# The entry of the first layer: constants cut up, x's norm from a token-major copy, products of ones during the load

## The chip, the cores and the metric

The kernel runs on one core of a Trainium2 chip. The metric is the device time of one execution in microseconds, lower is better. TensorE multiplies, VectorE (DVE), ScalarE (ACT) and GpSimd (POOL) work on vectors, SyncE (SP) issues the DMAs that move data between HBM and the on-chip memory.

## What is computed

Two blocks of a network over 256 tokens of width 2048, in f32. The entry, which the change touches, is the first block's norm and input product (`a_w_in`), a causal convolution of width 4, and the gated recurrence's decay, whose constants come from `a_lam`. The second block uses softmaxed bounds from `hgrn_lb_logits`, and conditions `silu(c)`, `silu(c_ctx)`.

```python
u = x * lax.rsqrt(mean(x * x, -1) + 1e-6) * norm_pre     # first block's norm
xb, gate = split(u @ a_w_in)                             # 2048 -> 2 x 2048
xc = causal_conv(xb, conv_w) + conv_b                    # width 4
r, i = sigmoid(block_matmul(xc, w_r) + b_r), sigmoid(block_matmul(xc, w_i) + b_i)
log_a = -8 * softplus(-lam) * r                          # decay of the recurrence
...                                                      # scan, gate, output, second block
mod = silu(c) @ w_mod + b_mod;  lb = softmax(hgrn_lb_logits)
```

## The kernel before

Activations lie feature-major: 128 features on the partitions, 256 tokens along, 16 such tiles for x (`XT`). A weight comes in blocks of 128 x 1024 (512 KB) into a ring of seven (`WF`), loaded by SP in the order of use. Each block is split in two: ScalarE rounds it to the high part (`WH`, function `high`), VectorE subtracts for the low part (`WL`, `low_part`); four buffers each. The moving operand is split the same way (`UX`, by `make`). TensorE does three products for each tile of 128 x 128: high x high, high x low, low x high. A WF buffer is free for its next load when VectorE has made the low part (`w_lo`); WH and WL are free when TensorE has finished the block (`prod`). Below, a block's number counts from 0 in the order of use: WL 4 is the low part of block 4.

One list of steps, made by `timetable()`, is walked by each engine's program; an engine takes from it what is its own, in order, and semaphores hold it where another's result is needed. Between two engines nothing else sets the order. The list begins with the loads of x in five pieces between weights, then the parameters and constants (`load_params`).

The first product is a quad: the first four output tiles of `xb` together, over blocks 0 to 7, two tiles of x for each block (`linear_quad`). x is multiplied by the gain `norm_pre` alone; the norm's factor 1/rms of each token, `RX` (the same on all partitions), is applied when an output tile is evacuated: `tt(XB, ps, RX, mult)` by VectorE. So no evacuation can be done before RX, and tile xb 4 needs the bank of the quad's first tile. Then follow xb 4 and xb 5 (blocks 8 to 11), the gates' products (blocks 12, 13), xb 6 (blocks 14, 15), with four products of a modulation block (`in_mod`, operand `SM`) ahead of it. Each xb tile has, after its evacuation, an activation on ScalarE (the fourth convolution tap and bias), three taps on VectorE, and a split for the gates (`XCs`).

RX before: in the quad's steps `x_square`, ScalarE squares four tiles of x at a time (128 x 1024), GpSimd adds the four to one (`XPARTS`), and in the step `("recip", "x")` TensorE multiplies ones with the four sums, which adds over features and spreads the sum to all partitions; ScalarE takes the root, VectorE the reciprocal of 128 x 256.

Small constants before: `small_params`, a background task of VectorE and ScalarE, in steps after the quad. It makes the softplus of -lam with a series (`nsp`, `psp`) and the softmaxed bounds (`lb`, `oml`), all on 128 x 16. In the step `conditions` ScalarE takes the sigmoid of `c` and VectorE multiplies (`cf`). ScalarE loads a table of functions when the function asked for is not in the present one.

Of the kernel before, what the change touches and what calls it, by code (L numbers as in the profile page):

```python
# [25 lines left out]
    ("norm_pre", 16), ("norm_post", 16), ("conv_w", 64), ("conv_b", 16), ("b_r", 16), ("b_i", 16),  # L26
    ("lam", 16), ("c", 16), ("cc", 16), ("b_mod", 96), ("npm", 16), ("nqm", 16), ("npl", 16),
    ("nql", 16), ("dw_w", 31 * 8), ("dw_b", 8), ("ln_g", 8), ("ln_b", 8), ("lb", 32), ("hng", 8),
]
PCOL = {}  # L30
_at = 0
for _n, _w in PARAMS:
# [8 lines left out]
    ["x", "y1", "x2", "ctx", "cmean", "cvar", "ro0", "ro1", "ro2", "ro3", "y2", "x3", "out"])}  # L41
# [5 lines left out]
PARTS_OF = {"small_params": 6, "recurrence": 16, "prepare_ctx": 26, "conv_branch": 46, "conv_split": 8,  # L47
# [17 lines left out]


# [3 lines left out]
def timetable():  # L70
# [287 lines left out]
    def linear_quad(kind, js):  # L358
# [14 lines left out]
        for b in range(8):  # L373
# [35 lines left out]
    for kind, j in order:  # L409
# [151 lines left out]
def build(nc, ctx, ins, out):  # L561
# [7 lines left out]
    def sem(name):  # L569
# [31 lines left out]
    ones_ok, c_sig, cf_ok, x_sq, x_part, mk_ok = (  # L601
        sem(n) for n in ("ones_ok", "c_sig", "cf_ok", "x_sq", "x_part", "mk_ok"))
# [69 lines left out]
    XT, CT, PT, BIG = area(0, 16), area(24, 16), area(56, 2), area(64, 16)  # L672
# [8 lines left out]
    XPARTS = area(82, 4)  # L681
# [32 lines left out]
    warm = small(4)  # L714
# [50 lines left out]
    ST = {"x": (RX, T, D), "y1": (RSTD[0], T, D), "x2": (RSTD[0], T, D), "ctx": (RC, T, D), "cvar": (SQ[1], T, 1024),  # L765
# [11 lines left out]
    def sync_program(sync):  # L777
# [3 lines left out]
        for what, *a in steps:  # L781
            if what == "start":
                n = PCOL["norm_pre"] + 16
                sync.dma_start(PR[:, 0:n], ins["params"][:, 0:n]).then_inc(s_gain, 16)
# [3 lines left out]
            elif what == "load_params":  # L788
                n = PCOL["norm_pre"] + 16
                sync.dma_start(PR[:, n:], ins["params"][:, n:]).then_inc(s_par, 16)  # L790
                sync.dma_start(CN[:, :], ins["consts"]).then_inc(s_par, 16)
            elif what == "load":
                i = a[0]
                b = blocks[i]
                if i >= NF:
                    w.wait_ge(*freed(i - NF))
                sync.dma_start(WF[:, i % NF, :], ins[b["name"]][b["index"]][:, b["lo"]:b["lo"] + BLK]).then_inc(
                    landed[i % NF], 16)
            elif what == "load_late":
                w.wait_ge(st_rs, RECIP["x"])  # L800
# [21 lines left out]
    def tensor_program(tensor):  # L822
# [70 lines left out]
        def stat(name):  # L893
            n = STAT[name]
            w.wait_ge(st_sq, n - 1)
            if name == "x":
                w.wait_ge(ones_ok, 1)
                for q in range(4):
                    w.wait_ge(x_part, q + 1)
                    i = mm(bank[7][:, 0:T], ONES[:, :], XPARTS[:, q, :], q == 0, q == 3)  # L900
            elif name == "ctx":
# [15 lines left out]
            i.then_inc(st_mm, 1)  # L917

# [148 lines left out]
        for what, *a in steps:  # L1067
# [8 lines left out]
            elif what == "stat" or (what == "recip" and a[0] == "x"):  # L1076
# [10 lines left out]
    def scalar_program(scalar):  # L1087
# [50 lines left out]
        def square(group, ft, src):  # L1138

            if ft == 0:  # L1140
                w.wait_ge(st_sq, {0: STAT["x"], 1: STAT["y1"], 2: STAT["ro3"], 3: STAT["y2"]}[group])
# [161 lines left out]
        def small_params(_):  # L1303
            w.wait_ge(sp_v, 1)
            act(el, al, ACT.Exp, scale=-1.0).then_inc(sp_a, 1)
            for _ in range(4):
                yield
            w.wait_ge(sp_v, 2)
            act(le, le, ACT.Exp).then_inc(sp_a, 1)
            yield  # L1310
            yield

# [128 lines left out]
        for what, *a in steps:  # L1441
# [8 lines left out]
            elif what == "bg":  # L1450
                name = a[0]
                if a[1] == 1:
                    running[name] = {
                        "small_params": small_params, "recurrence": recurrence, "prepare_ctx": prepare_ctx,
# [26 lines left out]
            elif what == "start":  # L1481
                w.wait_ge(ones_ok, 1)
                act(warm[:, 0:1], ONES[:, 0:1], ACT.Sqrt)
            elif what == "x_square":
                q = a[0]
                for k in range(4 * q, 4 * q + 4):
                    w.wait_ge(s_x[piece_of(k)], 16)
                act(BIG[:, 4 * q:4 * q + 4, :], XT[:, 4 * q:4 * q + 4, :], ACT.Square).then_inc(x_sq, 1)
            elif what == "conditions":
                w.wait_ge(s_par, 32)  # L1490
                act(cs, PR[:, PCOL["c"]:PCOL["c"] + 32], ACT.Sigmoid).then_inc(c_sig, 1)

    def vector_program(vector):
# [150 lines left out]
        def evac(what):  # L1644
            kind, j = what
            ps, leave = psum(what), left(what)[0]
            if kind == "xb":
                w.wait_ge(*full(what))
                w.wait_ge(st_rs, RECIP["x"])
# [109 lines left out]
        def small_params(_):  # L1759
            w.wait_ge(s_par, 32)  # L1760
            mark(ts(nl, lam, -1.0, None, ALU.mult))
            marked()
            tt(al, nl, lam, ALU.max).then_inc(sp_v, 1)
            w.wait_ge(sp_a, 1)
            mark(ts(sl, el, 2.0, None, ALU.add))
            marked()
            mark(vector.reciprocal(sl, sl))
            yield
            marked()
            mark(tt(sl, sl, el, ALU.mult))  # L1770
# [416 lines left out]
```

## Time and profile before

| | us |
|---|---|
| median of 3 runs | 2148.67 |
| lowest, highest | 2148.39, 2149.68 |
| span of the profiled execution | 2146.7 |
| TensorE busy in it | 2101.1 (98%) |
| VectorE, ScalarE, GpSimd busy | 1592.8, 1026.9, 99.5 |

The profiled execution is one of its own; its time is given as the span from its first instruction to its last. A line of a timeline gives the start, the time from there to the end of the group, engine and source line, the operation with output <- inputs, the number of instructions merged, and in brackets how long the engine stood idle before and what ended that. A window's last three numbers are the granted TensorE clock as a share of 2.4 GHz, DMA's busy share, and GB/s.

### The profile page before, as it was taken

How to read it: one execution, taken by the hardware profiler on the slowest of the kernel's cores; microseconds unless marked ns; L12 is line 12 of the kernel's file. 1: busy time of each engine (PE TensorE's matmuls, PEld its weight loads, DVE VectorE, ACT ScalarE, POOL GpSimd, SP SyncE). 2: the span in 40 equal slices, each digit the busy share in tenths (PEclk: the TensorE clock that was granted, in tenths of full speed). 3: DMA queues.
4: the chain of work that ended last, by engine and by line, in shares of the span. 5: the costliest groups of instructions: out<-in, count | busy, mean ns of one | idle time of the engine just before them, and what ended most of it. 6: DMA issues, size and time to landing. Idle time of an engine off the chain costs nothing.

```text
span 2146.7 us, 31802 instructions
## 1 busy us (share of the span) xinstructions
PE 2101.1 (98%) x12800; PEld 1830.9 (85%) x12800; DVE 1592.8 (74%) x2357; ACT 1026.9 (48%) x1560; POOL 99.5 (5%) x81
## 2 busy tenths in 40 slices
PE   7999999999999999999999999999999999999997
PEld 7787799787888888899999888878888888888886
DVE  7778699698889777667877898576766766656655
ACT  5766344556532322555554455554444434434443
POOL 1000002020000000000000001210000000000012
PEclk9999999999999999999999999999999999999998
DMA  6556778676733567444346988645775765555552
GB/s 232 197 200 224 249 253 274 223 273 230 247 111 130 172 234 267 149 132 141 132 135 207 367 300 300 228 146 195 258 254 187 240 230 196 181 192 196 187 178 97
DMA packets 122402, 447.80 MB, mean 209 GB/s; under 512 B 13712, under 2 KB 13840, under 8 KB 121872
## 3 DMA queue, kind: packets, MB, share of 16 engines
q1 hardware_dynamic: 122256, 445.78, 61.1%
q8 instruction: 101, 1.65, 0.3%
q14 instruction: 45, 0.37, 0.1%
HBM read 441.53 MB, written 4.19 MB: 208 GB/s over the span
## 4 chain that ended last, share of the span: by engine, by line
PE 71%; DVE 2%; ACT 1%; issue 1%; POOL 0%; POOLq 0%; DVEq 0%; ACTq 0%
PE bank L826 70%; DVE WL L1499 0%; DVE AR L1506 0%; PE bank L955 0%; DVE SR L1506 0%; PE bank L986 0%; ACT WH L1093 0%; DVE AR L1499 0%; POOL AR L2102 0%; ACT AR L1094 0%; ACT AR L1093 0%; DVE AR L1599 0%; ACT SR L1094 0%; POOL AR L2104 0%; ACT L1094 0%
## 5 line engine op out<-in xcount | busy, mean ns | idle before, releaser
L826 PE MATMUL bank<-SR,WH 128*128 128x512 f32 (+1 forms) x6880 | 1811.5, 352 | 28.6 <-DVE WL L1499 10.7
L826 PE MATMUL bank<-SR,WL 128*128 128x256 f32 (+1 forms) x5088 | 1208.7, 288 | 0.5 <-DVE SR L1506 0.4
L826 PEld LDWEIGHTS bank<-SR,WH 128*128 128x128 f32 x6880 | 1096.0, 190 | 94.0 <-issue 30.6
L826 PEld LDWEIGHTS bank<-SR,WL 128*128 128x128 f32 x5088 | 963.7, 190 | 156.1 <-DVE SR L1506 1.9
L1499 DVE TENSOR_TENSOR WL<-WF,WH 128x1024 fp32r<-128x1024 f32 x636 | 774.6, 1229 | 221.2 <-ACT WH L1093 221.0
L1093 ACT ACTIVATE WH<-WF 128x1024 fp32r<-128x1024 f32 x636 | 671.6, 1057 | 463.4 <-PE bank L826 428.0
L1093 ACT ACTIVATE AR<-bank 128x256 f32<-128x256 f32 (+2 forms) x261 | 103.6, 407 | 277.8 <-PE bank L826 263.4
L1506 DVE SCALAR_TENSOR_TENSOR AR<-WF,SM,AR 128x512 f32<-128x512 f32 (+1 forms) x240 | 232.8, 1000 | 4.5
L1499 DVE TENSOR_TENSOR AR<-AR 128x256 f32<-128x256 f32 (+9 forms) x374 | 154.8, 445 | 58.4 <-ACT AR L1094 35.4
L2097 POOL TENSOR_TENSOR AR<-AR 128x256 f32<-128x256 f32 x56 | 74.2, 1325 | 2013.1 <-ACT AR L1094 2012.8
L1499 DVE TENSOR_TENSOR AR<-AR,bank 128x256 f32<-128x256 f32 x112 | 47.2, 421 | 119.2 <-PE bank L826 91.2
L1094 ACT ACTIVATE AR<-AR 128x256 f32<-128x256 f32 (+3 forms) x152 | 75.1, 499 | 96.3 <-DVE AR L1499 81.3
L1499 DVE TENSOR_TENSOR AR<-bank,AR 128x256 f32<-128x256 f32 (+1 forms) x200 | 86.0, 432 | 39.9 <-PE bank L826 18.0
L1506 DVE SCALAR_TENSOR_TENSOR AR<-AR,PR 128x255 f32<-128x255 f32 (+21 forms) x200 | 89.1, 448 | 6.0
L1093 ACT ACTIVATE SR<-AR 128x256 fp32r<-128x256 f32 (+1 forms) x138 | 56.5, 419 | 71.5 <-DVE AR L1499 64.6
L1094 ACT ACTIVATE AR<-bank 128x256 f32<-128x256 f32 x74 | 26.6, 382 | 118.8 <-PE bank L826 118.7
L826 PE MATMUL bank<-WF,SM 128*2 128x512 f32 x160 | 73.4, 592 | 0.0
L1499 DVE TENSOR_TENSOR SR<-AR,SR 128x256 fp32r<-128x256 f32 (+1 forms) x138 | 58.9, 435 | 16.4 <-ACT SR L1093 15.7
L826 PE MATMUL bank<-AR 128*128 128x128 f32 (+1 forms) x416 | 64.0, 297 | 2.8 <-issue 2.3
L826 PEld LDWEIGHTS bank<-AR 128*128 128x128 f32 x416 | 56.7, 191 | 5.0 <-issue 2.7
L826 PEld LDWEIGHTS bank<-WF,SM 128*2 128x2 f32 x160 | 11.2, 84 | 39.6 <-issue 36.3
L1506 DVE SCALAR_TENSOR_TENSOR AR<-AR 128x256 f32<-128x256 f32 x88 | 37.3, 423 | 8.8 <-ACT AR L1094 6.6
(75 smaller groups left out, 464.0 us busy)
## 6 DMA issues: line engine op xcount, KB each, us to landing
WF<-in_mlp SPq DMA_DIRECT2D x256, 512.0 KB, 4.2
WF<-in_mod SPq DMA_DIRECT2D x192, 512.0 KB, 4.9
WF<-in_w_in SPq DMA_DIRECT2D x176, 512.0 KB, 4.3
WF<-in_a_in SPq DMA_DIRECT2D x64, 512.0 KB, 4.7
WF<-in_a_out SPq DMA_DIRECT2D x32, 512.0 KB, 5.1
WF<-in_ple_g SPq DMA_DIRECT2D x32, 512.0 KB, 4.5
WF<-in_w_out SPq DMA_DIRECT2D x32, 512.0 KB, 5.6
WF<-in_pw SPq DMA_DIRECT2D x16, 512.0 KB, 3.2
```

The lines of the kernel that those rows point to most:

```text
L826: return tensor.matmul(o, l, r, start=start, stop=stop, skip_group_check=True)
L1093: return scalar.activation(o, x, f, scale=scale)
L1094: return scalar.activation(o, x, f, scale=scale, bias=bias)
L1499: return vector.tensor_tensor(o, a, b, op)
L1506: return vector.scalar_tensor_tensor(o, a, s, b, op1, op2)
L2097: pool.tensor_tensor(ACC, ACC, SQ[ft % 2], ALU.add).then_inc(acc, 1)
```

## The change

- `PARAMS` is reordered: gain, `c`, `cc`, `lam` and `lb` come first, and the first parameter load brings 96 columns (48 KB) instead of 16 (8 KB).
- `small_params` is gone as a task. `small(0)` stands at the start, ahead of the first split, with both exponentials on ScalarE there; `small(1)` to `small(6)` stand between the quad's blocks 0 to 5.
- x comes a second time, token-major (`xR`, 128 x 4096, 2 MB), loaded in the quad's first block step. ScalarE squares each half with a sum along the row (`accum_out`, 128 x 2048) in the steps of blocks 5 and 6. A new step `x_scale` behind the quad: root of 128 x 2 on ScalarE, reciprocal of 128 x 2 on VectorE, two products on TensorE of the factor, repeated, with the identity, which spread it to all partitions, and a copy to RX on ScalarE.
- GpSimd's eight additions, the four products with ones, the root and the reciprocal of 128 x 256 are gone.
- At the start TensorE multiplies ones by ones 14 times (128 x 128, f32, `WARM`).
- The table of the exponential is loaded first, the root's ahead of the first square, the sigmoid's at `conditions`, and it stays for the gates. The product `cf` moves behind xb 4 (`conditioned`).

```diff
-            background.append(("small_params", 0))
...
+                if b == 0:
+                    steps.append(("load_xr",))
+                if b < 6:
+                    steps.append(("small", b + 1))
+                if b in (5, 6):
+                    steps.append(("x_square", b - 5))
-                if b < 4:
-                    steps.append(("x_square", b))
-                if b == 6:
-                    steps.append(("recip", "x"))
...
+        if kind == "xb":
+            steps.append(("x_scale",))
...
+            if j == 4:
+                steps.append(("conditioned",))
...
+        def x_wider():                                   # TensorE
+            w.wait_ge(x_inv, 1)
+            w.wait_ge(s_par, 32)
+            for h in range(2):
+                r = xinv[:, h:h + 1]
+                r = bass.AP(tensor=r.tensor, offset=r.offset, ap=[r.ap[0], [0, P]])
+                i = mm(bank[7][:, h * P:h * P + P], r, ident, True, True)
+            i.then_inc(x_wide, 1)
...
+            elif what == "start":                        # TensorE
+                w.wait_ge(ones_ok, 1)
+                for _ in range(WARM):
+                    mm(bank[7][:, 0:P], ONES[:, :], ONES[:, :], True, True)
...
-                act(warm[:, 0:1], ONES[:, 0:1], ACT.Sqrt)
+                act(warm[:, 0:1], ONES[:, 0:1], ACT.Exp)
+                w.wait_ge(sp_v, 1)
+                act(el, al, ACT.Exp, scale=-1.0)
+                act(le, le, ACT.Exp).then_inc(sp_a, 1)
...
+                h = a[0]                                 # x_square, ScalarE
+                if h == 0:
+                    act(warm[:, 4:5], ONES[:, 0:1], ACT.Sqrt)
+                w.wait_ge(s_xr, 16)
+                scalar.activation(XR[:, h, :], XR[:, h, :], ACT.Square, scale=1.0, bias=0.0,
+                                  accum_out=xsum[:, h:h + 1]).then_inc(x_sq, 1)
+            elif what == "x_scale":
+                w.wait_ge(s_par, 32)
+                w.wait_ge(x_sq, 2)
+                act(xsum, xsum, ACT.Sqrt, scale=1.0 / D, bias=eps).then_inc(x_root, 1)
+                w.wait_ge(x_wide, 1)
+                act(RX, bank[7][:, 0:T], ACT.Copy).then_inc(x_rs, 1)
...
-                w.wait_ge(st_rs, RECIP["x"])             # VectorE, evacuation of xb
+                w.wait_ge(x_rs, 1)
...
+            elif what == "x_scale":                      # VectorE
+                w.wait_ge(x_root, 1)
+                vector.reciprocal(xinv, xsum).then_inc(x_inv, 1)
```

VectorE behind the quad. `SM` are the small constants, `AR` with `PR` a convolution tap (its width 255, 254 or 253), `WL` a low part, `AR<-bank,AR` an evacuation. Before:

```order
L1502 TENSOR_SCALAR SM<-SM 128x16
L1506 SCALAR_TENSOR_TENSOR SM<-SM 128x16 x8
L1502 TENSOR_SCALAR SM<-SM 128x16
L1506 SCALAR_TENSOR_TENSOR SM<-SM 128x16
L1502 TENSOR_SCALAR SM<-SM 128x16 x2
L1499 TENSOR_TENSOR SM<-PR 128x16
L1499 TENSOR_TENSOR SM<-PR,SM 128x2x8
L1499 TENSOR_TENSOR WL<-WF,WH 128x1024
L1506 SCALAR_TENSOR_TENSOR AR<-AR,PR 128x255
```

Now, at the same low part and on:

```order
L1526 SCALAR_TENSOR_TENSOR AR<-AR,PR 128x253
L1519 TENSOR_TENSOR WL<-WF,WH 128x1024
L1526 SCALAR_TENSOR_TENSOR AR<-AR,PR 128x255
L1526 SCALAR_TENSOR_TENSOR AR<-AR,PR 128x254
L1526 SCALAR_TENSOR_TENSOR AR<-AR,PR 128x253
L1526 SCALAR_TENSOR_TENSOR AR<-AR,PR 128x255
L1526 SCALAR_TENSOR_TENSOR AR<-AR,PR 128x254
L1526 SCALAR_TENSOR_TENSOR AR<-AR,PR 128x253
L1519 TENSOR_TENSOR AR<-bank,AR 128x256
L1519 TENSOR_TENSOR SM<-SM,PR 128x32
L1519 TENSOR_TENSOR WL<-WF,WH 128x1024
```

The constants are gone from between the taps and WL 11, and `cf` (`SM<-SM,PR 128x32`) now stands behind the evacuation of xb 4.

ScalarE from the end of the quad. `SR<-AR,PR` casts a tile of x, `WH` is a high part, `AR<-bank,CN` the root of the sum, `AR<-AR,PR ... x4` the four convolution activations. Before:

```order
L1093 ACTIVATE SR<-AR,PR 128x256 x2
L1093 ACTIVATE WH<-WF 128x1024
L1094 ACTIVATE AR<-bank,CN 128x256
L1093 ACTIVATE WH<-WF 128x1024
L1094 ACTIVATE AR<-AR,PR 128x256 x4
L1094 ACT_TABLE_LOAD
L1094 ACTIVATE SM<-PR 128x32
L1093 ACTIVATE WH<-WF 128x1024
L1094 ACT_TABLE_LOAD
L1094 ACTIVATE SM<-SM 128x16
```

Now:

```order
L1113 ACT_TABLE_LOAD
L1113 ACTIVATE SM<-ONES 128x1
L1504 ACTIVATE AR,SM<-AR 128x2048
L1112 ACTIVATE SR<-AR,PR 128x256 x2
L1112 ACTIVATE WH<-WF 128x1024
L1504 ACTIVATE AR,SM<-AR 128x2048
L1112 ACTIVATE WH<-WF 128x1024
L1113 ACTIVATE SM<-SM,CN 128x2
L1112 ACTIVATE AR<-bank 128x256
L1113 ACTIVATE AR<-AR,PR 128x256 x4
L1113 ACT_TABLE_LOAD
L1113 ACTIVATE SM<-PR 128x32
```

A table load and two squares of 128 x 2048 now stand in this stretch, and the table load behind `SM<-PR 128x32` is gone.

SP, from the last piece of x. Before:

```order
L787 DMA AR<-in_xT 128x1024
L790 DMA PR<-in_params 128x648
L791 DMA CN<-in_consts 128x132
L797 DMA WF<-in_a_in 128x1024 x7
L797 DMA WF<-in_a_gates 128x1024 x2
```

Now:

```order
L795 DMA AR<-in_xT 128x1024
L797 DMA PR<-in_params 128x568
L798 DMA CN<-in_consts 128x132
L804 DMA WF<-in_a_in 128x1024 x4
L807 DMA AR<-in_xR 128x4096
L804 DMA WF<-in_a_in 128x1024 x3
```

The 2 MB of xR stand between blocks 8 and 9 on the same queue.

## Rows read from the trace of the kernel before

**Rows 1.** Windows: length, busy us (instructions) of each engine, clock, DMA.
```profile
0.00:75.00 75.00, 57.86 (x398) 52.79 (x399) 52.83 (x96) 48.99 (x78) 10.23 (x13) 0.95 0.60 209
75.00:2147.00 2072.00, 2043.27 (x12405) 1778.13 (x12403) 1540.00 (x2261) 977.94 (x1483) 89.24 (x68) 1.00 0.61 209
```

**Rows 2.** Waits of TensorE, 0 to 75: us in total, times, longest.
```profile
PE bank L826 <- DVE WL L1499: 7.5, 5, 3.6
```

**Rows 3.** Timeline, TensorE, 50 to 72: start, us, work, count, idle before.
```profile
50.98 0.80 PE L826 MATMUL bank<-SR,WH 128*128 128x256 f32 x2 [3.63 <-DVE WL L1499]
...
57.12 0.48 PE L826 MATMUL bank<-SR,WH 128*128 128x256 f32 x2 [0.65 <-DVE SR L1499]
...
60.94 0.50 PE L826 MATMUL bank<-SR,WH 128*128 128x256 f32 x2 [1.43 <-DVE AR L1499]
...
64.66 0.47 PE L826 MATMUL bank<-SR,WH 128*128 128x256 f32 x2 [0.94 <-DVE WL L1499]
...
70.57 1.88 PE L826 MATMUL bank<-WF,SM 128*2 128x512 f32 x4
```

**Rows 4.** Windows, 52 to 54, all engines.
```profile
52.00:54.00 2.00, 2.00 (x11) 2.00 (x11) 1.80 (x5) 0.09 (x1) 0.00 (x0) 0.50 0.77 242
```

**Rows 5.** Timeline, VectorE, 38 to 61.
```profile
38.75 0.42 DVE L1499 TENSOR_TENSOR AR<-bank,AR 128x256 f32<-128x256 f32 x1 [0.29 <-PE bank L826]
41.38 0.19 DVE L1499 TENSOR_TENSOR SM<-SM,PR 128x32 f32<-128x32 f32 x1 [2.21 <-ACT SM L1094]
...
42.63 2.95 DVE L1506 SCALAR_TENSOR_TENSOR AR<-AR,PR 128x255 f32<-128x255 f32 x6
45.49 0.17 DVE L1502 TENSOR_SCALAR SM<-PR 128x16 f32<-128x16 f32 x1
...
49.71 1.22 DVE L1499 TENSOR_TENSOR WL<-WF,WH 128x1024 fp32r<-128x1024 f32 x1
...
53.70 0.17 DVE L1499 TENSOR_TENSOR SM<-PR,SM 128x16 f32<-128x16 f32 x1
...
55.42 1.22 DVE L1499 TENSOR_TENSOR WL<-WF,WH 128x1024 fp32r<-128x1024 f32 x1
...
60.47 0.42 DVE L1499 TENSOR_TENSOR AR<-bank,AR 128x256 f32<-128x256 f32 x1
```

**Rows 6.** Timeline, ScalarE, 37 to 66.
```profile
37.05 2.76 ACT L1094 ACTIVATE AR<-AR,PR 128x256 f32<-128x256 f32 x4
...
62.79 1.28 ACT L1094 ACT_TABLE_LOAD   x1
64.09 1.57 ACT L1094 ACTIVATE AR<-bank,PR 128x256 f32<-128x256 f32 x4
```

**Rows 7.** Timeline, VectorE, 8 to 14.
```profile
8.66 0.88 DVE L1506 SCALAR_TENSOR_TENSOR SR<-AR,PR,SR 128x256 fp32r<-128x256 f32 x2
11.23 2.08 DVE L1506 SCALAR_TENSOR_TENSOR SR<-AR,PR,SR 128x256 fp32r<-128x256 f32 x2 [1.70 <-ACT SR L1093]
13.23 1.21 DVE L1499 TENSOR_TENSOR WL<-WF,WH 128x1024 fp32r<-128x1024 f32 x1
```

**Rows 8.** DMA issues at 3.06 and 14.47 (KB, us to landing); window 15 to 20.
```profile
AR<-in_xT SPq DMA_DIRECT2D x1, 512.0 KB, 7.0
...
WF<-in_a_in SPq DMA_DIRECT2D x1, 512.0 KB, 8.5
...
15.00:20.00 5.00, 3.87 (x32) 3.67 (x32) 4.38 (x4) 2.58 (x5) 2.11 (x2) 1.00 1.04 408
```

**Rows 9.** Groups by form, ScalarE: busy us, mean ns, idle before.
```profile
L1093 ACT ACTIVATE WH<-WF 128x1024 fp32r<-128x1024 f32 x636 | 671.6, 1057 | 463.4 <-PE bank L826 428.0 <-DMA WF<-in_w_out 14.5 <-DMA WF<-in_ple_g 8.9
...
L1093 ACT ACTIVATE SR<-AR,PR 128x256 fp32r<-128x256 f32 x16 | 7.2, 494 | 3.0 <-DMA AR<-in_xT 3.0
...
L1094 ACT ACTIVATE AR<-AR 128x2048 f32<-128x2048 f32 x2 | 3.8, 1917 | 6.7 <-DVE AR L1502 5.9 <-DVE AR L1499 0.9
```

**Rows 10.** Timeline, TensorE, 31 to 33: the products with ones.
```profile
31.07 1.89 PE L826 MATMUL bank<-AR,ONES 128*128 128x256 f32 x8
```

More of the change, by code:

```diff
@@ L40 @@
 STAT = {n: i + 1 for i, n in enumerate(
-    ["x", "y1", "x2", "ctx", "cmean", "cvar", "ro0", "ro1", "ro2", "ro3", "y2", "x3", "out"])}
+    ["y1", "x2", "ctx", "cmean", "cvar", "ro0", "ro1", "ro2", "ro3", "y2", "x3", "out"])}
 RECIP = {n: i + 1 for i, n in enumerate(n for n in STAT if n != "cmean")}
@@ L712, in build @@
     gsc, gscc, gga, gsf, ggf = (small(16) for _ in range(5))
-    warm = small(4)
+    warm = small(5)
+    xsum, xinv = small(2), small(2)
     def bank_of(what):
@@ L895, in stat @@
             w.wait_ge(st_sq, n - 1)
[L896 to L901, printed above, removed]
+            if name == "ctx":
                 w.wait_ge(cx_v, 1)
@@ L1075, in tensor_program @@
                 next(running[name], None)
-            elif what == "stat" or (what == "recip" and a[0] == "x"):
+            elif what == "start":
[3 more added lines that the diff above has]
+            elif what == "x_scale":
+                x_wider()
+            elif what == "stat":
                 stat(a[0])
@@ new lines, in small @@
+            if n == 0:
+                w.wait_ge(s_gain, 16)
+                mark(ts(nl, lam, -1.0, None, ALU.mult))
+                mark(tt(lm3, l4[:, :, 0, :], l4[:, :, 1, :], ALU.max))
+                marked()
+                tt(al, nl, lam, ALU.max)
+                tt(le4[:, :, 0, :], l4[:, :, 0, :], lm3, ALU.subtract)
+                tt(le4[:, :, 1, :], l4[:, :, 1, :], lm3, ALU.subtract).then_inc(sp_v, 1)
+            elif n == 1:
+                w.wait_ge(sp_a, 1)
+                mark(ts(sl, el, 2.0, None, ALU.add))
+                mark(tt(lb3, le4[:, :, 0, :], le4[:, :, 1, :], ALU.add))
+                marked()
+                vector.reciprocal(sl, sl)
+                mark(vector.reciprocal(lb, lb))
+            elif n == 2:
+                tt(sl, sl, el, ALU.mult)
+                mark(tt(lb3, lb3, le4[:, :, 0, :], ALU.mult))
+                marked()
+                tt(s2, sl, sl, ALU.mult)
+                mark(ts(oml, lb, -1.0, 1.0, ALU.mult, ALU.add))
+            elif n == 3:
+                mark(ts(ql, s2, 1.0 / 17, None, ALU.mult))
+                marked()
+                mark(stt(ql, ql, 1.0 / 15, s2, ALU.add, ALU.mult))
+                marked()
+                mark(stt(ql, ql, 1.0 / 13, s2, ALU.add, ALU.mult))
+            elif n == 4:
+                for k in (5, 4, 3):
+                    mark(stt(ql, ql, 1.0 / (2 * k + 1), s2, ALU.add, ALU.mult))
+                    marked()
+            elif n == 5:
+                for k in (2, 1):
+                    mark(stt(ql, ql, 1.0 / (2 * k + 1), s2, ALU.add, ALU.mult))
+                    marked()
+                ts(nl, nl, 0.0, None, ALU.max)
+                mark(stt(ql, ql, 1.0, sl, ALU.add, ALU.mult))
+            else:
+                mark(stt(ql, ql, 2.0, nl, ALU.mult, ALU.add))
+                marked()
+                ts(nsp, ql, -8.0, None, ALU.mult)
+                ts(psp, ql, 8.0, None, ALU.mult).then_inc(sp_ok, 1)
@@ L2058, in vector_program @@
                 vector.tensor_copy(MK[:, :, :], MF).then_inc(mk_ok, 1)
-            elif what == "conditions":
+            elif what == "conditioned":
                 w.wait_ge(c_sig, 1)
                 tt(cf, cs, PR[:, PCOL["c"]:PCOL["c"] + 32], ALU.mult).then_inc(cf_ok, 1)
+            elif what == "start":
+                small(0)
+            elif what == "small":
+                small(a[0])
+            elif what == "x_scale":
+                w.wait_ge(x_root, 1)
+                vector.reciprocal(xinv, xsum).then_inc(x_inv, 1)
             elif what == "finish":
```

111 lines of the change are left out of this document (27 added, 84 removed).

## The prediction

> **What bounds the kernel now.** First the windows [rows 1]: after 75 us TensorE is busy 2043.27 of 2072 us, 98.6%, so what is off TensorE there costs little. Before 75 us it is busy 57.86 of 75, and all of the change lies there. Then the waits of TensorE in that stretch [rows 2]: the split of the weights' low parts (WL, VectorE) holds it five times for 7.5 us, the longest 3.6. In order of time [rows 3], with a weight's block at 2.9 us (48 matmuls of xb 6 from 64.66 to 70.57, so 24 in 2.95, nearer 2.88 without the ends): 3.63 us of idleness before 50.98, 0.65 before 57.12, 1.43 before 60.94, 0.94 before 64.66. Behind the longest of them the granted clock is 0.50 [rows 4], the 1.2 GHz level: the block that starts at 50.98 takes until about 56.5, 2.6 us more than at 2.4 GHz.
>
> Why WL is late is read from VectorE's queue [rows 5]. It has evacuated the quad's last tile at 39.2 and then stands 2.21 us until 41.38, behind the product cf, which waits for ScalarE's sigmoid, itself behind four activations (2.76 us, until 39.8) and the load of a table, 1.28 us [rows 6]. Then come a WL and six convolution taps, and from 45.49 to 49.71, 4.22 us, nothing but 16-column operations on constants: a chain of about twenty instructions, each waiting for the one before. Only then WL for the block that TensorE wants, which begins at 49.71. From 53.70 to 55.08 (it ends with the evacuation ahead of 55.42, 0.34 us) another 1.38 us of constants. TensorE at 60.94 follows the evacuation that VectorE began at 60.47, to 0.05 us: here VectorE's queue is the path, and TensorE follows it.
>
> **The constants.** They are cut into seven pieces that stand between the splits of the quad. Out of the stretch from 39.2 to 55.42 (16.2 us) go 2.21 + 4.22 + 1.38 = 7.8 us; cf moves behind the evacuation of xb 4, its sigmoid then long done, and costs 0.1 there. In their new places six pieces of two to four operations cost VectorE 0.6 to 0.9 us each (4.22 us for 19 operations is 0.2 each). Below I count them where they stand. ScalarE's two exponentials move ahead of the first x piece, for which it waits until about 5.2 now, and the constants' first piece needs about 1 us after a load of 48 instead of 8 KB, so I take 0 and at most 0.5.
>
> **The entry to the quad.** GpSimd's eight sums go. While one ran, two of VectorE's 256-column operations took 2.08 us instead of 0.88 [rows 7], and the second WL began at 13.23. Without the sums and without ScalarE's four squares of 1.04 us, those two operations follow x's third piece (landed at 3.06 + 7.0 = 10.1 [rows 8]), so WL 1 ends near 12.7 (before: 14.4). Next in turn: WL 2 at 16.7, WL 4 at 22.7, WL 5 at 23.8. Blocks on TensorE then end at 15.6, 19.6, 22.5, 25.6 (block 4), 28.5, 31.4 and 34.3 (block 7). The four f32 products with ones, 1.89 us on TensorE [rows 10], are no longer there; with them and the later waits block 7 ended at about 38.4. The fourteen products of ones at the start last 14 x 0.43 = 6.0 us at 1.2 GHz (0.43 is a quarter of 1.89 us doubled for the clock and halved for 128 columns), from 0.95 to 7.0, before TensorE's first weight at 7.53. They let block 0 end at 10.5 instead of 12.9; block 1 starts at 12.7 either way, so I give them 0.2 us. If the clock falls again in the new pause, block 1 takes 2.9 us more, ends at 18.5 and moves block 2 by 1.8 us; the next waits swallow most of that.
>
> **x's scale, the new path.** xR is 2 MB on the queue that weights use. It is issued behind the ninth weight block, which landed at 14.47 + 8.5 = 23.0 in a stretch at 408 GB/s [rows 8]; the same bytes stand ahead of it, so xR lands at 23.0 + 2.10 MB / 408 = 28.1. The weights behind it land 5.1 us later, the tenth at 28.1 + 1.3 = 29.4, wanted at 30.8: covered. ScalarE's queue, with WH at 0.95 from start to start and two x casts 0.8 [rows 9]: WH 8 waits for block 4 and starts at 25.65; table load 1.28 [rows 6] and a one-column root to 28.0; square with sum over 2048 columns 28.15 to 30.0 (a plain square of 2048 takes 1.92 [rows 9], the sum itself I price at 0, upper bound 0.3 each); casts of x 14 and 15 to 30.8, in time for block 7 at 31.4; WH 9 to 31.75; second square to 33.6; WH 10 to 34.55; root 34.75. VectorE's reciprocal to 35.05, two products with the identity 0.6, a copy 0.4: RX is ready at 36.15. TensorE stands from 34.3 to 35.1 for the reciprocal and from 35.7 to 36.65 for the first evacuation. The first evacuation thus starts at 36.2; before it was four evacuations back from 39.2, at 36.6. All that the quad gained on TensorE, 4 us, shrinks to 0.4 here.
>
> The Trainium skill speaks against the table load in that chain: *ScalarE: Activation LUTs*, section "What ACT_TABLE_LOAD costs", gives 1.28 us and a drain of 1.38 us on top. The trace has no such drain: the load of 1.28 us at 62.79 is followed by an activation that starts at 64.09 [rows 6]. By the page the chain would end 1.4 us later; I keep the row.
>
> **The sum.** From 36.2 VectorE does four evacuations back to back (0.34 each, 1.35; before they were paced by TensorE, 2.6), a WL 1.15, six taps 2.9, and meets WH 11: ScalarE needs 2.76 + 1.29 + 0.1 + 1.05 for four activations, the sigmoid's table, the sigmoid and WH, from 36.65 to 41.85; VectorE is there at 41.6 and waits 0.25. WL, six taps, one evacuation and cf: WL 12 starts at 46.25, before at 55.42 [rows 5]. That is 9.2 us. From there to 60.94 both kernels have the same queue, so TensorE resumes at 51.75. TensorE's own work allows it: from 36.65 four blocks end at 48.2, and it wants VectorE's next cast at 48.1. Last, the 0.94 us before 64.66. The row names a WL [rows 3], but that one ended at 63.7; the product also needs a bank that ScalarE frees, whose first sigmoid starts at 64.09 and ends at 64.5, behind a table load at 62.79 [rows 6]. I read it as that. The sigmoid's table is now in place, the load goes, and TensorE resumes as soon as its four products of 1.88 us end at 63.72: 0.94 us more. Together 10.1 us; the 3.63 and the 0.50 clock are part of it, not to be added. What is late next: evacuations again, then ScalarE's recurrence around 70 to 85, which moves by 10.5 us along with TensorE, and where TensorE is fully busy. Span 2146.7 - 10.1 = 2136.6. The median of the runs is 2148.67, 2.0 above the span: 2138.6.
>
> **Rivals.**
> (a) *xR comes late.* Each microsecond by which it lands after 28 passes to the end whole, since the sum hangs on RX from there. For it: it shares the queue; against it: the stretch ran at 408 GB/s. At 200 GB/s it lands at 33.5 and the gain is 4.7: 2144. The sums and the drain of the page, if they exist, are of this kind, 0.3 to 2 us: 2139 to 2141.
> (b) *The gain is given back.* TensorE, 10 us ahead, would meet a wait it did not have: weights behind xR (needs landing over 1.4 us later than I have for the tenth block), or ScalarE at 70 to 85, where it is busy all the time. A gain under 4.3 us: 2145 to 2149.
> (c) *Slower.* One mechanism: RX is so late that ScalarE, which waits in order for xR, holds up the casts and WH 9 behind it; TensorE starves at block 7, falls to 1.2 GHz for some 5.5 us as after 50.98 and loses 2.7 us more. Loss begins when xR lands later than 28 + 10.1 - 2.7 = 35.5, a transfer below 170 GB/s. At 40: 2153. Nothing in the rows points there.
> (d) *More.* If WL 1 and WL 2 come earlier than I have them, ScalarE's chain starts earlier, but xR bounds it at 28.1: at most 0.5. If TensorE's later idleness (29 us after 75) also shrinks, up to 3: 2135.5.
> (e) *The warm-up does nothing.* As worked out, 0.2 us at most; no case of its own.
>
> **How the numbers follow.** Forecast (gain 8.5 to 11.5) 0.66; (d) 0.07; (a) with a gain of 4.3 to 8.5: 0.18; (b) 0.06; (c) 0.03. A measurement of this kernel can tell about 0.2%, 4.3 us, from no change. Faster by that: 0.66 + 0.07 + 0.18 = 0.91; within: 0.06; slower: 0.03. Range: 2135.5, the end of (d), to 2143.0, xR at 32.5; that leaves out (b), (c) and the tail of (a).
>
> **What would show it.** In the profile after: no idle stretch of TensorE over 2 us after 20 us and granted clock 1.00 from 45 to 60; xR landing near 28; RX's copy near 36; WL 12 on VectorE at 46.2; TensorE's first evacuation wait in the gates ending at 51.75 and the mod products of xb 6 directly followed by its weights near 54.5. Wrong would be: the copy of RX after 38, a wait of TensorE for WH or WL between 20 and 34, or a new wait at 60 to 75.

## The result

The changed kernel takes 2139.28 us (median of 4 runs, 2139.09 to 2139.71) where the one before, beside it, takes 2149.18 (4 runs, 2148.39 to 2150.12). The ratio is 0.9953, 95% interval 0.9939 to 0.9967. The profiled execution's span fell from 2146.7 to 2137.2 us, 9.5 us; 10.1 were forecast, and the time of 2138.6 was missed by 0.7. Nearly everything was at its place. The experiments show how the gain divides: the constants and the sigmoid's table bring most of it, as the forecast had it (8.7 of 10.1 us), and the new norm by itself brings nothing that the medians show, which the forecast did not say.

The same two windows as in [rows 1], of the changed kernel:

```profile
0.00:75.00 75.00, 67.86 (x488) 61.70 (x489) 51.56 (x109) 53.82 (x87) 0.41 (x5) 0.98 0.72 261
75.00:2147.00 2072.00, 2033.74 (x12339) 1770.15 (x12337) 1532.72 (x2248) 971.61 (x1474) 88.78 (x68) 0.99 0.61 208
```

TensorE is busy 10.0 us more of the first 75, 5.7 of which are the products of ones (first row below), and 9.5 us less behind them, where the stretch simply ends earlier. Its longer idle stretches up to 60 us, as in [rows 3]:

```profile
0.99 5.69 PE L835 MATMUL bank<-ONES 128*128 128x128 f32 x28 [0.99 <-POOL ONES L2103]
...
13.22 0.80 PE L835 MATMUL bank<-SR,WH 128*128 128x256 f32 x2 [3.11 <-DVE WL L1519]
...
35.95 0.71 PE L835 MATMUL bank<-CN,SM 128*128 128x128 f32 x4 [0.87 <-DVE SM L2087]
37.75 0.48 PE L835 MATMUL bank<-SR,WH 128*128 128x256 f32 x2 [1.09 <-DVE AR L1519]
...
52.45 0.50 PE L835 MATMUL bank<-SR,WH 128*128 128x256 f32 x2 [0.79 <-DVE AR L1519]
...
53.36 1.88 PE L835 MATMUL bank<-WF,SM 128*2 128x512 f32 x4
55.17 0.50 PE L835 MATMUL bank<-SR,WH 128*128 128x256 f32 x2
```

The 3.63 us before 50.98 are gone; what is left of the gates' waits is 0.79 before 52.45, where before 60.94 it was 1.43. The product of xb 6 follows the modulation's products without a pause, at 55.17 instead of 64.66: 9.49 us, the whole difference of the spans. VectorE, whose queue is the path ([rows 5] of before):

```profile
35.73 0.17 DVE L2087 RECIPROCAL SM<-SM 128x2 f32<-128x2 f32 x1 [1.22 <-ACT SM L1113]
37.18 1.42 DVE L1519 TENSOR_TENSOR AR<-bank,AR 128x256 f32<-128x256 f32 x4 [1.29 <-ACT AR L1112]
38.52 1.21 DVE L1519 TENSOR_TENSOR WL<-WF,WH 128x1024 fp32r<-128x1024 f32 x1
39.65 2.94 DVE L1526 SCALAR_TENSOR_TENSOR AR<-AR,PR 128x255 f32<-128x255 f32 x6
...
46.84 0.18 DVE L1519 TENSOR_TENSOR SM<-SM,PR 128x32 f32<-128x32 f32 x1
46.94 1.22 DVE L1519 TENSOR_TENSOR WL<-WF,WH 128x1024 fp32r<-128x1024 f32 x1
```

WL 12 starts at 46.94 instead of 55.42. ScalarE, on the new path to RX:

```profile
26.35 1.06 ACT L1112 ACTIVATE WH<-WF 128x1024 fp32r<-128x1024 f32 x1 [1.02 <-PE bank L835]
27.43 1.28 ACT L1113 ACT_TABLE_LOAD   x1
28.72 0.20 ACT L1113 ACTIVATE SM<-ONES 128x1 f32<-128x1 f32 x1
28.91 1.91 ACT L1504 ACTIVATE AR<-AR 128x2048 f32<-128x2048 f32 x1
30.73 0.19 ACT L1504 ACTIVATION_READ_ACCUMULATOR AR<-AR 128x1 f32 x1
...
35.41 0.28 ACT L1113 ACTIVATE SM<-SM,CN 128x2 f32<-128x2 f32 x1
36.70 0.38 ACT L1112 ACTIVATE AR<-bank 128x256 f32<-128x256 f32 x1 [1.00 <-PE bank L835]
```

**A mark far behind the entry.** From 75 us on TensorE's waits are alike in both kernels. One of them, 1.78 us long, stands in every trace at about 1300 us, and the time at which TensorE resumes there tells what the entry has brought, without what comes later. Before and after:

```profile
1302.81 0.47 PE L826 MATMUL bank<-SR,WH 128*128 128x512 f32 x1 [1.79 <-issue]
```

```profile
1293.30 0.47 PE L835 MATMUL bank<-SR,WH 128*128 128x512 f32 x1 [1.78 <-issue]
```

That is 9.51 us. Below this is called the mark. In three executions of the changed kernel it stood at 1293.30, 1293.33 and 1293.73, with the first evacuation within 0.07 us (37.18, 37.13, 37.11): in the third the clock from 37 to 60 us was 0.93 instead of 1.00. So a difference of two marks under about 0.4 us says nothing by itself. Each mark below is that of one execution.

### The profile page after: what moved, and what is told of

It is laid out like the page before. It is cut to its first block, busy times and chain, and to the rows that moved or that the text cites. A ratio compares the mean times of both kernels' runs of the same rounds, so it can differ in the third digit from the quotient of the medians.

```text
span 2137.2 us, 31842 instructions
## 1 busy us (share of the span) xinstructions
PE 2101.6 (98%) x12824; PEld 1831.8 (86%) x12824; DVE 1584.3 (74%) x2357; ACT 1025.4 (48%) x1561; POOL 89.2 (4%) x73
## 4 chain that ended last, share of the span: by engine, by line
PE 71%; DVE 2%; ACT 1%; issue 1%; POOL 0%; POOLq 0%; ACTq 0%; DVEq 0%
PE bank L835 70%; DVE WL L1519 0%; DVE AR L1526 0%; DVE SR L1526 0%; PE bank L968 0%; ACT WH L1112 0%; PE bank L999 0%; DVE AR L1519 0%; POOL AR L2122 0%; ACT AR L1113 0%; ACT AR L1112 0%; DVE AR L1619 0%; ACT SR L1113 0%; POOL AR L2124 0%; ACT L1113 0%
## 5 line engine op out<-in xcount | busy, mean ns | idle before, releaser
L1113 ACT ACTIVATE AR<-AR 128x256 f32<-128x256 f32 (+2 forms) x148 | 70.9, 484 | 97.3 <-DVE AR L1519 82.5
L835 PEld LDWEIGHTS bank<-WF,SM 128*2 128x2 f32 x160 | 11.2, 84 | 39.6 <-issue 36.3
```

Source lines behind the costliest of these rows:

```text
L835: return tensor.matmul(o, l, r, start=start, stop=stop, skip_group_check=True)
L1113: return scalar.activation(o, x, f, scale=scale, bias=bias)
```

## The experiments

They were run in three groups, each on one chip, and each ratio is to the kernel before in the same group. The changed kernel itself was in two of the groups: 2138.93 us (4 runs, 2138.01 to 2141.37; before 2149.74) and 2139.55 (5 runs, 2139.07 to 2140.15; before 2148.30). Two variants, the table loaded once more and GpSimd's additions put back, have one execution each, so for them there is no median.

**The changed kernel again, in the first and in the last group:**

> The changed kernel again, beside the three that follow, so that they are compared on the same chip. 2139.3 within 0.4; ratio to before 0.9955.

> The changed kernel again, as the reference of this call: 2138.5 to 2139.7.

The ratios are 0.9951 (0.9937 to 0.9966) and 0.9958 (0.9944 to 0.9971), the marks 1293.73 and 1293.33. The profiled execution of the first has a span of 2139.2, 2 us more than the other's 2137.4; the last part of this section comes back to that. It is also the slowest run of its group, 2141.37 in time, and lies outside the 0.4 that was expected.

**The products of ones.**

```diff
-WARM = 14
+WARM = 0
```

> The changed kernel without the fourteen products of ones. Theory: they bring nothing, since block 1 waits for WL 1 (13.2 us) in either case and RX waits for xR. In the trace of the changed kernel the clock fell back to 1.2 GHz in the pause of 3.1 us before 13.22, so without them block 0 runs at 1.2 GHz (ends near 12.3) and block 1 at 2.4 GHz (ends near 16.1 instead of 17.4); both are absorbed by xR. Same time within 0.3 us as the changed kernel. Rival: the warm clock is worth the 3 us that block 0 is shorter: 2142.

Measured 2139.20 us (4 runs, 2138.57 to 2139.76) beside 2138.93, ratio 0.9951 (0.9936 to 0.9966), mark at 1293.52. Without the ones block 0 runs at half the clock, its first 16 products in 3.75 us instead of 2.18, and block 1 still starts at 13.12 instead of 13.22, as WL 1 sets it:

```profile
7.41 3.75 PE L835 MATMUL bank<-SR,WH 128*128 128x256 f32 x16 [7.41 <-ACT WH L1112]
...
13.12 0.64 PE L835 MATMUL bank<-SR,WH 128*128 128x256 f32 x2 [0.25 <-DVE WL L1519]
```

The ones bring nothing: what they save in block 0 becomes the 3.11 us of waiting. In the first execution of the changed kernel the products behind that pause run at the lower clock, until about 16 us, as these windows show; the last columns are the granted clock, DMA's share and GB/s:

```profile
10.00:15.00 5.00, 1.89 (x9) 1.78 (x9) 2.72 (x8) 4.17 (x7) 0.00 (x0) 0.77 1.01 406
15.00:20.00 5.00, 5.00 (x40) 5.00 (x40) 3.32 (x7) 1.91 (x3) 0.00 (x0) 0.89 1.04 412
```

That fall is not what makes the ones useless. In the execution with the mark at 1293.73 the clock stayed at 1.00 behind a pause of 3.00 us; TensorE then waited 0.42 us for the next WL, and the first evacuation came no earlier (37.11), since the squares waited for xR.

**The constants and the sigmoid's table alone.** Put on the kernel before: the reordered parameters, the seven pieces of `small`, the exponentials and their table at the start, `cf` behind xb 4. The norm stays with ScalarE's squares, GpSimd's sums, the products with ones and the root of 128 x 256.

```diff
+                if b < 6:
+                    steps.append(("small", b + 1))
                 if b < 4:
                     steps.append(("x_square", b))
+                if b == 4:
+                    steps.append(("root_table",))
...
-                background.append(("small_params", 0))
...
+            if j == 4:
+                steps.append(("conditioned",))
```

> The kernel before with the constants alone moved: seven pieces in the quad, exponentials first, the root's table loaded after block 4, the sigmoid's kept for the gates; norm by GpSimd and products with ones as before, no xR, no ones. Theory: the constants carry 7.8 us and the table 0.9, so 8.5 to 9.3 us under before, span near 2137.9, time near 2140; VectorE starts WL 12 near 47.6. Rival: the quad's entry needed the rebuilt norm to have room on VectorE for the pieces, and block 7 ends 2 us or more later than 38.5: gain of 6 to 7.

Measured 2139.56 us (4 runs, 2139.54 to 2140.39), ratio 0.9954 (0.9937 to 0.9970): in the median all but 0.6 us of the change's gain (2138.93 beside it), and within its spread. By the mark, 1294.63, it is 8.2 of 9.5 us: WL 12 starts at 48.21 instead of 55.42, 7.2 us earlier, and the 0.94 before xb 6 is gone. What 7.2 lacks to 7.8 is lost in the quad: three operations of the constants (27.01, 1.13 us) stand ahead of a split for which TensorE waits 0.77 us, its block starts at 28.81 instead of 28.12, and the last evacuation at 39.44 instead of 38.75 [rows 5].

```profile
37.66 0.77 DVE L1498 TENSOR_TENSOR AR<-bank,AR 128x256 f32<-128x256 f32 x2
...
39.44 0.42 DVE L1498 TENSOR_TENSOR AR<-bank,AR 128x256 f32<-128x256 f32 x1 [0.29 <-PE bank L830]
39.78 1.22 DVE L1498 TENSOR_TENSOR WL<-WF,WH 128x1024 fp32r<-128x1024 f32 x1
```

The first evacuation is 0.48 us later than in the changed kernel, and the four take 2.12 us to the next WL instead of 1.34, as TensorE is still finishing the quad's tiles. Together 1.26 us: that is what the new norm, with the ones and without GpSimd's additions, adds here (1.3 at the mark).

**The norm alone.** The reverse: the changed kernel with `small_params` as a background task, the tables and the exponentials as before. xR, the new scale and the ones stay.

```diff
-                if b < 6:
-                    steps.append(("small", b + 1))
...
+                background.append(("small_params", 0))
...
-            if j == 4:
-                steps.append(("conditioned",))
...
-                act(warm[:, 0:1], ONES[:, 0:1], ACT.Exp)
+                act(warm[:, 0:1], ONES[:, 0:1], ACT.Sqrt)
```

> The changed kernel with the constants made as before, as a task behind the quad, with their exponentials there; xR, the rebuilt norm and the ones stay. Theory: RX and the first evacuation stay near 37.2 (before 36.6), cf waits for the sigmoid until 41.3 as before, and 4.2 + 1.4 us of constants stand in VectorE's queue again, so TensorE waits before WL 11 until about 51 and the whole gain is gone: 2148.5 to 2150. Rival: the rebuilt norm is worth something of its own by TensorE's four microseconds in the quad: 2145 or less.

Measured 2148.38 us (10 runs) beside 2148.64 (19 runs), ratio 0.9999 (0.9990 to 1.0008). The mark is at 1302.22, 0.6 earlier than before. The expectation held, and its rival (2145 or less) did not. VectorE shows why so little is left:

```profile
36.76 1.42 DVE L1523 TENSOR_TENSOR AR<-bank,AR 128x256 f32<-128x256 f32 x4 [1.29 <-ACT AR L1109]
40.87 0.19 DVE L1523 TENSOR_TENSOR SM<-SM,PR 128x32 f32<-128x32 f32 x1 [2.69 <-ACT SM L1110]
```

The evacuations are done a microsecond earlier than before, and `cf`, behind them, waits for ScalarE's sigmoid 2.69 us instead of 2.21 [rows 5]. Half of the microsecond is left: WL 12 starts at 54.90 for 55.42. The old queue swallows the rest of what the new norm gives. Marks of the two halves add to 8.8 of 9.5 us.

**The table loaded once more.** The changed kernel, with an exponential that nobody needs behind xb 4, so that the sigmoid's table must be loaded again ahead of the gates' sigmoids.

```diff
+            elif what == "conditioned":
+                act(warm[:, 0:1], ONES[:, 0:1], ACT.Exp)
```

> The changed kernel with one activation of the exponential on ScalarE after xb 4 is evacuated, which costs a table load in ScalarE's idle time there and makes the sigmoid's table load return ahead of the gates' first sigmoid. Theory: TensorE resumes after the modulation products 0.7 to 0.95 us later than in the changed kernel, whose blocks follow them without a pause; span 0.7 to 0.95 longer, if the clock does the same elsewhere. Rival: the wait there was for WL 14, as the trace's releaser says: no change.

One execution: span 2139.3, mark 1295.55, 2.25 us later. Two waits of TensorE make it up:

```profile
53.74 0.51 PE L835 MATMUL bank<-SR,WH 128*128 128x256 f32 x2 [2.11 <-DVE AR L1521]
...
57.46 0.47 PE L835 MATMUL bank<-SR,WH 128*128 128x256 f32 x2 [0.93 <-DVE WL L1521]
```

The first is a side effect of the extra exponential (1.28 us of table load ahead of a WH, so 1.29 later than 52.45). The second is the pause of 0.94 us before 64.66 [rows 3] come back, 0.93 us. As in [rows 3] the row names a WL, yet that WL ended at 56.44, a microsecond before TensorE resumed. What ends just before 57.46 is the first sigmoid, behind its table:

```profile
55.59 1.28 ACT L1113 ACT_TABLE_LOAD   x1
56.89 1.57 ACT L1113 ACTIVATE AR<-bank,PR 128x256 f32<-128x256 f32 x4
```

**GpSimd's additions put back.** The changed kernel, with eight additions of GpSimd on an area that nobody uses (zeroed at the start), released by the same splits as before.

```diff
+        for q in range(4):
+            w.wait_ge(n_hi, (4, 6, 10, 12)[q])
+            pool.tensor_tensor(J[:, 0:2, :], J[:, 2:4, :], J[:, 4:6, :], ALU.add).then_inc(p_own, 1)
+            w.wait_ge(p_own, 2 * q + 2)
+            pool.tensor_tensor(J[:, 6, :], J[:, 0, :], J[:, 1, :], ALU.add).then_inc(p_own, 1)
```

> The changed kernel with eight additions on GpSimd of the sizes of before, on an area of zeros, released by the casts of x 3, 5, 9 and 11. Their sums go nowhere. Theory: VectorE's paired operations under them take about 2.1 us instead of 0.9 and a WL 2.3 instead of 1.2, TensorE's blocks 1 to 6 come up to 3 us later, and RX, bound by xR, stays within 1 us of 37.1: the end moves by under 1 us. Rival: the removed sums are a term of the gain: 2 us or more.

One execution: span 2138.1, mark 1295.15. VectorE's first evacuation is at 39.05, 1.87 us later than 37.18, and the mark 1.85 later: they are one and the same. The span is only 0.9 longer, since the stretch behind the mark was 1.0 shorter here. While GpSimd adds, VectorE's operations take longer (the last two rows are a GpSimd addition and ScalarE's first square):

```profile
12.01 2.29 DVE L1519 TENSOR_TENSOR WL<-WF,WH 128x1024 fp32r<-128x1024 f32 x1
...
21.98 4.01 DVE L1519 TENSOR_TENSOR WL<-WF,WH 128x1024 fp32r<-128x1024 f32 x2
25.91 2.12 DVE L1526 SCALAR_TENSOR_TENSOR SM<-SM 128x16 f32<-128x16 f32 x3
...
24.98 2.17 POOL L2110 TENSOR_TENSOR AR<-AR 128x512 f32<-128x512 f32 x1
...
30.80 1.90 ACT L1504 ACTIVATE AR<-AR 128x2048 f32<-128x2048 f32 x1
```

against 1.22, 2.35 and 0.59 us in the changed kernel. The Trainium skill (*GPSIMD Engine Reference*, "Specifications") says that GpSimd's interfaces to the on-chip memory are shared with VectorE, with contention where VectorE runs in a 2-port mode or has two inputs from there; these rows agree, and show it for 16 columns too. The time added does not grow with the size of the operation: 1.07 us for a WL, 1.53 for three operations of 16 columns, which begin under an addition that lasts until 27.15. That VectorE stands still until GpSimd's addition is over fits these rows; it was not tested by itself.

WL 1's end moves by 1.1 us, TensorE's block 4 and with it WH 8 by 2.0 (28.32 for 26.35), and the squares behind it by 1.9. Only the 1.1 is VectorE's delay. TensorE, which has no pause from there to the end of block 4, takes 0.8 us more for blocks 1 to 4 because the lower clock lasts longer: 0.61 from 16 to 20 us, where the changed kernel had 0.99. So 1.85 is what this one execution shows, and another draw of the clock may give less.

The expectation, that xR's landing would hide this, was wrong: the squares in the changed kernel start at 28.91, when both xR (28.9) and the queue of ScalarE (28.92, end of the table load and its activation) release them. In the execution of the changed kernel in which the clock stayed up, ScalarE's queue was 0.4 us ahead of xR, no more:

```profile
28.85 1.91 ACT L1504 ACTIVATE AR<-AR 128x2048 f32<-128x2048 f32 x1 [0.42 <-DMA AR<-in_xR]
```

**xR later, twice.** Its load issued behind three more of the quad's steps, or behind one:

```diff
-                if b == 0:
+                if b == 3:
                     steps.append(("load_xr",))
```

> The changed kernel with xR's load three blocks later in the list (behind the load of block 11 or 12 instead of 8). Theory (a) of the prediction: xR lands near 33 instead of 28.9, the casts of x 14 and 15 and WH 9 stand behind the square that waits for it, block 7 starts late, TensorE may fall to 1.2 GHz, and RX comes 4.1 to 5.5 us later; all of it passes to the end: 2143.4 to 2145. Rival: later waits swallow it, since TensorE waits for evacuations anyway: under 1 us.

```diff
-                if b == 0:
+                if b == 1:
                     steps.append(("load_xr",))
```

> The changed kernel with xR's load issued two weight blocks later. It should land some 2 to 4 us later than 28.9, near 31 to 33. Theory (each microsecond by which xR lands later passes to the end whole, and without a threshold): the first evacuation and WL 12 move by the same 2 to 4 us, and so does the median, to 2141 to 2143. Rival: small delays are swallowed, as the 1.3 us of the version with the constants alone were, and only a delay that starves TensorE before the quad's end counts: under 1 us in the median.

ScalarE with the landing at 36.1, and then with the landing at 31.0:

```profile
36.13 1.91 ACT L1504 ACTIVATE AR<-AR 128x2048 f32<-128x2048 f32 x1 [5.86 <-DMA AR<-in_xR]
```

```profile
31.02 1.91 ACT L1504 ACTIVATE AR<-AR 128x2048 f32<-128x2048 f32 x1 [1.90 <-DMA AR<-in_xR]
```

| | squares start | first evacuation | mark | median us |
|---|---|---|---|---|
| before | | 36.59 | 1302.81 | 2148.3 to 2149.7 |
| changed kernel | 28.91 | 37.18 | 1293.30 | 2138.93, 2139.55 |
| one step later | 31.02 | 39.66 | 1295.83 | 2142.07 (5 runs, ratio 0.9969, 0.9956 to 0.9981) |
| three steps later | 36.13 | 44.81 | 1300.96 | 2148.35 (10 runs, ratio 0.9997, 0.9988 to 1.0007) |

The mark moves with the first evacuation, by 2.53 for 2.48 and by 7.66 for 7.63, without a threshold. The evacuation itself moves by 0.4 us more than the squares (2.48 for 2.11, 7.63 for 7.22): TensorE begins block 7 after a pause of 1.89 or 5.84 us, runs it in part at the lower clock (0.87 and 0.66 from 35 to 45 us), and is not done when the reciprocal is, so that the copy of RX waits 1.39 or 1.43 us for the two products instead of 1.00. The landing of 36.1 was later than the 33 that the expectation had: SP met a full ring on its way to the load and issued it at 27.06, behind block 13, and not behind 11 or 12. So the size expected was missed and the mechanism held. At this landing the median is that of the kernel before.

**The scale earlier.** The root's table ahead of block 5's activations; xR in two loads of 1 MB, each with its own semaphore; the second square and the root ahead of the last splits of the quad, the reciprocal too; the two products with the identity within block 7; the sigmoid of the conditions behind xb 4's high parts.

```diff
+                if b == 4:
+                    steps.append(("root_table",))
+                if b == 5:
+                    steps.append(("x_square", 0))
...
+            if kind == "xb" and b == 6:
+                steps.append(("x_square", 1))
+                steps.append(("x_root",))
...
+                    if kind == "xb" and b == 7 and i == 4:
+                        steps.append(("x_scale",))
...
+        if kind == "xb" and j == 4:
+            steps.append(("conditions",))
```

> The changed kernel with x's scale made earlier: xR in two loads with a semaphore each, the root's table loaded after block 4, second square, root and reciprocal ahead of WH 9, the two spreading products in the middle of block 7, the sigmoid of c behind WH 12. Theory (everything from RX to the gates hangs on RX): RX near 35.3 instead of 37.1, WL 12 about 2 us earlier, time 1.7 to 2.2 us under the changed kernel, 2137.3. Rival: WH 9 and WH 10 come later and TensorE waits for them, or VectorE's queue is the bound: same time as the changed kernel.

Measured 2137.92 us (4 runs, 2137.01 to 2139.21) beside 2138.93, ratio 0.9945 (0.9931 to 0.9960), first evacuation at 34.94, mark 1291.10. These runs overlap with the changed kernel's. The same version was run again, this time without the ones:

> The changed kernel with the root's table, the second square, the root and the reciprocal moved ahead of the quad's end (the version measured at 2137.92 against 2138.93 for the change) and, in addition, without the 14 products of ones at the start. Theory: the ones bring nothing and the earlier scale is worth what its gates start earlier, 2.2 us in the one profiled execution, so RX's copy near 34.5, WL 12 near 44.7, and the median 1 to 2.2 us below the changed kernel of the same call. Rival: the gain of that version is one execution's luck with the clock, and the medians agree within 0.5 us.

Measured 2135.93 us (5 runs, 2135.80 to 2136.94) beside 2139.55 (5 runs, 2139.07 to 2140.15); the ratio to before is 0.9942 (0.9930 to 0.9955). The first evacuation is at 34.45 and the mark at 1290.62, 2.7 us earlier than the changed kernel's both. This version beats both kernels. It is 3.6 us faster than the changed one, where 1 to 2.2 were expected, and no run of one overlaps with the other's. It changes two things at once; the ones alone, taken out above, moved the median by 0.3 us in the other direction, so the earlier scale is taken as the cause. Its ScalarE and VectorE:

```profile
27.01 1.90 ACT L1509 ACTIVATE AR<-AR 128x2048 f32<-128x2048 f32 x1
...
31.79 0.29 ACT L1120 ACTIVATE SM<-SM,CN 128x2 f32<-128x2 f32 x1
31.99 2.00 ACT L1119 ACTIVATE WH<-WF 128x1024 fp32r<-128x1024 f32 x2
33.89 0.39 ACT L1119 ACTIVATE AR<-bank 128x256 f32<-128x256 f32 x1
```

```profile
34.45 1.41 DVE L1527 TENSOR_TENSOR AR<-bank,AR 128x256 f32<-128x256 f32 x4
```

There is no idle time ahead of the copy of RX or of the evacuations. Of the 3.6 us in the medians the mark holds 2.7; the rest is behind it.

**What lies behind the mark.** From the mark to the end of the span it is 843.9 us before and after, but 842.8 with the constants alone, 843.0 in the fastest version, and 845.5 with xR three steps later (845.6 one step later), and also in one execution of the changed kernel. The work there is the same. The clock is not; windows of the changed kernel, of the constants alone, and of xR three steps later, each around two pauses of TensorE (1.8 and 4.0 us):

```profile
1280.00:1320.00 40.00, 38.22 (x222) 33.15 (x221) 34.78 (x47) 21.31 (x35) 2.91 (x2) 1.00 0.77 269
1380.00:1420.00 40.00, 35.91 (x164) 25.43 (x163) 27.59 (x46) 18.24 (x31) 8.71 (x8) 0.91 0.39 126
```

```profile
1280.00:1320.00 40.00, 38.23 (x222) 33.20 (x221) 34.78 (x47) 21.41 (x36) 1.96 (x1) 1.00 0.74 261
1380.00:1420.00 40.00, 35.98 (x174) 25.84 (x173) 28.55 (x47) 19.59 (x35) 9.76 (x8) 0.96 0.40 133
```

```profile
1280.00:1320.00 40.00, 38.22 (x213) 33.10 (x212) 34.37 (x51) 20.73 (x35) 0.00 (x0) 0.96 0.73 245
1380.00:1420.00 40.00, 35.97 (x173) 26.20 (x172) 23.68 (x37) 18.24 (x33) 11.24 (x9) 0.91 0.40 133
```

The clocks are 1.00 and 0.91, 1.00 and 0.96, 0.96 and 0.91. A mean lower by 0.04 over 40 us is 3.2 us at half the clock, or 1.6 us of work not done, and 845.5 is 1.6 above 843.9. For 0.05 it would be 2.0, where 842.8 is 1.1 below: some of that low clock may fall where TensorE waits anyway. All 13 profiled executions fall into these three groups: 1.00 and 0.91 goes with 843.5 to 844.1 us, 1.00 and 0.96 with 842.8 to 843.0, 0.96 and 0.91 with 845.5 to 845.6. That is why the constants alone, 1.3 us late at the mark, end 0.2 us behind the changed kernel in the profiled executions. Whether an execution draws this by chance or by where its pauses fall is not settled: the changed kernel gave both 843.9 and 845.5.

## Why the prediction was right, step by step

- **The constants, 7.8 us out of VectorE's queue, and the sigmoid's table, 0.94.** Sum 8.7; alone they measured 8.2 at the mark, 7.2 and 0.9, the rest being the 0.7 us that a piece of the constants costs in the quad. Right, and they are most of the change: the prediction's order of the terms was right, but it did not say that the other half alone would bring nothing.
- **The entry.** WL 1 was forecast to end at 12.7 and ended at 13.08; WH 8 for 25.65 came at 26.35. The case that block 1 meets the low clock was named as a branch and occurred (0.77 in 10 to 15). It cost block 1 about 1.4 us (4.23 for 2.88), not 2.9, as the clock was back at about 16 us, and no later wait swallowed it before WH 8: TensorE shows no pause from 13.22 to the end of the quad. In the execution where the clock stayed up, the WL behind and xR took the saving instead.
- **The warm-up worth at most 0.2 us.** Right; nothing that can be measured. A product of ones was priced at 0.43 us, but a quarter of 1.89, doubled and halved, is 0.47; the 14 took 5.69 us, 0.41 each. Nothing hangs on it.
- **xR at 28.1.** It landed at 28.9 (issued at 13.57, 15.3 us), in a stretch at 412 GB/s where [rows 8] had 408. From there the chain ran as written: the root was forecast to start at 34.55 and started at 35.41, RX 36.15 and the first evacuation 36.2 came at 37.08 and 37.18. That is 0.6 us later than the 36.59 of before, where 0.4 earlier was forecast; the gain in the quad is only that the four evacuations now go back to back and the WL behind them can start at 38.52. Of the 0.98 us by which the first evacuation was late, 0.8 is the landing and ScalarE's queue, 0.2 the two reads of the sum, forecast with 0 and at most 0.3 each; each takes 0.19 and moves what is behind it by 0.09.
- **The drain of 1.38 us** that the Trainium skill (*ScalarE: Activation LUTs*, "What ACT_TABLE_LOAD costs") has for a table load is in no trace here: the load at 27.43 takes 1.28 and the next activation is at 28.72. The row was the right choice.
- **WL 12 at 46.25, TensorE at 51.75.** Came at 46.94 and 52.45, 0.7 late each. The first evacuation was 0.98 late, and 0.3 came back: the wait of 0.25 for WH 11 did not occur, as ScalarE's four activations took 2.08 us here where 2.76 was taken from [rows 6]. The old ones were paced by VectorE's evacuations.
- **0.94 us before xb 6.** Right to 0.01, and the reading of the row against its own releaser is confirmed by the table put back.
- **The span.** 9.49 us at 55.17, 9.51 at the mark, 9.5 at the end: rival (b), a gain given back later, did not occur. It has ScalarE busy all the time from 70 to 85; the trace of before shows 11.2 of 15 us. TensorE was the one busy throughout, 15.0 of 15, and in the changed kernel it is so from 60 to 85. The 10.5 us by which the sum lets ScalarE's recurrence move is a slip for 10.1.
- **Rival (a), each microsecond of xR's landing passes whole.** Confirmed twice, at 2.5 and at 7.6 us for landings 2.1 and 7.2 later. The prediction's own rows had ScalarE's queue ready at 28.0, beside xR at 28.1, but it priced only a late xR; a late queue costs the same. GpSimd's additions, gone, are worth up to 1.85 us for this reason, and by the rows of ScalarE an earlier xR alone would have brought 0 to 0.4 us (that was not run).
- **Rival (c), slower from a landing at 35.5 on.** The point holds in the medians (36.1: ratio 0.9997), but not by the mechanism given. Of the 2.7 us for TensorE's lower clock 0.4 are in the mark: the clock is 0.66 from 35 to 45 us there, yet all behind hangs on RX, and the mark is still 1.85 us ahead of before. In the profiled execution the rest of the loss lies behind the mark (845.5 us for 843.9).

## What to carry to other kernels

A vector engine's queue that TensorE follows to 0.05 us is the path, and short operations in it cost their whole chain; moving them to where TensorE is busy for other reasons, and keeping one table loaded, brought all but 1.3 of 9.5 us here. Two changes to one entry are not to be priced apart: either may stand behind the other (the new norm was worth 0.6 us with the old queue and 1.3 with the new one). And to tell what an edit at the start does, take a mark behind the entry, not the span: the clock after later pauses moved the span by 1.6 us between two executions of the changed kernel, and by up to 2.8 between all that were profiled. The mark has a spread of its own, 0.4 us here.

## What the runs showed of the hardware

- A sum along the row with an activation (`accum_out`) is a second instruction on ScalarE, ACTIVATION_READ_ACCUMULATOR, 0.18 to 0.19 us long, 0.09 from start to start.
- A pause of TensorE of about 3 us behind block 0 was followed by the low clock at once in two executions of the changed kernel (3.11 us, clock 0.50 from 13 to 16; 2.86 us, 0.53), and not at all in a third of the same program (3.00 us, 1.00).
- With GpSimd adding, VectorE's 128 x 1024 subtraction took 2.29 us instead of 1.22, and three operations on 16 columns 2.12 instead of 0.59. With the constants alone a single operation of 16 columns took 1.28 us instead of 0.17 (14.70 to 15.98), under a GpSimd addition that ran from 14.66 to 15.95.
